# Hybrid decoder layer: the first expert choice made for one head, eight candidates ahead, and the causal mask of the first two token tiles added by VectorE

## The reference, cut to what matters

```python
h = rms_norm(x, norm1_g); proj = h @ w_in
A = stick_breaking_attention(q, k, v)     # 8 heads x 64, strictly causal
B = gated_deltanet(...)                   # 4 heads x 128, chunked
x = x + concat(rms_norm(A), B) @ w_out
h = rms_norm(x, norm2_g)
# PEER: per token 8 heads, each picks 16 of 128*128 experts
s1, s2 = q1 @ keys1.T, q2 @ keys2.T       # 128 scores each
v1, i1 = top_k(s1, 16); v2, i2 = top_k(s2, 16)
score, pos = top_k(v1[:, None] + v2[None, :], 16)
expert = i1 * 128 + i2 (at pos); gate = softmax(score)
x = x + sum over 8*16 experts of gate * gelu(h . u[expert]) * v[expert]
```

## Time and profile before

| | us |
|---|---|
| median of 3 runs | 1650.77 (1649.88 to 1652.06) |
| profiled execution, own time | 1653.62 |
| its span, first to last instruction | 1651.7 |
| PE busy | 1357.4 (82%) |
| DVE busy | 1057.7 (64%) |
| POOL busy | 776.3 (47%) |
| ACT busy | 349.9 (21%) |
| gathers: 115776 packets, 536.92 MB | 80.6% of 16 DMA engines' span |

### The profile page before, as it was taken

How to read it: one execution, slowest core, us unless ns; L and a number is a source line. 1 busy time by engine, 2 the same in 40 slices (tenths; PEclk the granted TensorE clock), 3 DMA queues, 4 the chain that set the end, 5 groups by cost and what they waited for, 6 DMA issues and landing times.

```text
span 1651.7 us, 15972 instructions
## 1 busy us (share of the span) xinstructions
PE 1357.4 (82%) x5078; PEld 675.1 (41%) x5078; DVE 1057.7 (64%) x2839; ACT 349.9 (21%) x786; POOL 776.3 (47%) x848
## 2 busy tenths in 40 slices
PE   8999989888789887977859976677877787778877
PEld 7866574433346555643213320122333333333333
DVE  4625249957777889976555766444565666666646
ACT  2321432302242322011002120021122222222221
POOL 3000015766676657765557677445433333333331
PEclk8999999999999898987879898799989999998899
DMA  4223817999999999999999999999999999999995
GB/s 155 77 102 115 303 41 273 389 410 412 409 409 409 411 410 409 409 409 412 399 413 409 378 410 411 418 418 416 421 422 421 422 421 422 421 422 421 422 422 241
DMA packets 130211, 599.35 MB, mean 363 GB/s; under 512 B 15824, under 2 KB 15824, under 8 KB 97360
## 3 DMA queue, kind: packets, MB, share of 16 engines
q0 software_dynamic: 115776, 536.92, 80.6%
q1 hardware_dynamic: 14208, 61.15, 9.7%
q10 hardware_dynamic: 144, 0.26, 0.0%
HBM read 596.18 MB, written 2.10 MB: 362 GB/s over the span
## 4 chain that ended last, share of the span: by engine, by line
DMA 45%; PE 28%; DVE 10%; POOL 8%; issue 5%; ACT 3%; DVEq 1%; ACTq 0%; SPq 0%; POOLq 0%
DMA arena<-in_peer_uv,arena 19%; DMA arena<-in_peer_v,arena 16%; DMA arena<-in_peer_u,arena 10%; PE psum L1153 7%; DVE arena L1954 4%; POOL arena L741 4%; POOL arena L753 4%; PE psum L1131 4%; PE psum L1084 3%; PE psum L817 3%; PE psum L828 3%; PE psum L1065 1%; DVE arena L1554 1%; ACT arena L1444 1%; PE psum L932 1%
## 5 line engine op out<-in xcount | busy, mean ns | idle before, releaser
L1954 DVE CUSTOM_DVE_ANT_0 arena<-arena,psum 128x1024 f32<-128x1024 f32 x512 | 623.3, 1218 | 418.6 <-DMA arena<-in_peer_uv,arena 247.0
L1153 PE MATMUL psum<-arena 128*128 128x512 f32 x880 | 427.3, 644 | 95.2 <-ACT arena L1444 95.2
L741 POOL DMA_INDIRECT arena<-in_peer_u,arena x288 | 273.7, 950 | 360.2 <-PE psum L894 223.0
L1131 PE MATMUL psum<-arena 128*32 128x512 f32 x1152 | 278.3, 719 | 134.7 <-DMA arena<-in_peer_v,arena 134.5
L773 POOL DMA_INDIRECT arena<-in_peer_uv,arena x220 | 206.3, 938 | 333.5 <-PE psum L1153 294.7
L753 POOL DMA_INDIRECT arena<-in_peer_v,arena x288 | 271.8, 944 | 143.3 <-issue 76.6
L1153 PEld LDWEIGHTS psum<-arena 128*128 128x128 f32 x880 | 176.3, 205 | 350.6 <-issue 219.2
L1131 PEld LDWEIGHTS psum<-arena 128*32 128x32 f32 x1152 | 48.0, 119 | 317.0 <-DMA arena<-in_peer_v,arena 230.2
L817 PE MATMUL psum<-arena 128*128 128x512 f32 x256 | 117.1, 604 | 1.3 <-DVE st L1596 1.2
L828 PE MATMUL psum<-arena 128*128 128x256 f32 x384 | 97.0, 414 | 5.7 <-ACT arena L1212 4.2
L1084 PE MATMUL psum<-arena 128*128 128x512 f32 x224 | 100.5, 602 | 1.3 <-ACT arena L1371 1.3
(11 more groups left out here) (283 smaller groups left out, 1392.1 us busy)
## 6 DMA issues: line engine op xcount, KB each, us to landing
arena<-in_w_in SPq DMA_DIRECT2D x28, 1024.0 KB, 7.8
arena<-in_w_out SPq DMA_DIRECT2D x16, 512.0 KB, 7.9
arena<-in_peer_w_q SPq DMA_DIRECT2D x16, 512.0 KB, 14.1
arena<-in_peer_w_q SPq DMA_DIRECT2D x8, 1024.0 KB, 13.3
arena<-in_peer_u,arena POOLq DMA_INDIRECT x292, 15.2
arena<-in_peer_v,arena POOLq DMA_INDIRECT x292, 15.9
arena<-in_peer_uv,arena POOLq DMA_INDIRECT x220, 27.1
arena<-in_x SPq DMA_DIRECT2D x4, 512.0 KB, 5.0
```

The lines of the kernel that those rows point to most:

```text
L741: pool.indirect_dma_start(row, None, u_d, bass.IndirectOffsetOnAxis(ap=eid[i % 2][:, c:c + 1], axis=0)).then_inc(landed, 16)
L1131: mm = pe.matmul(bank[6 + half][group * UK:(group + 1) * UK], zrows[k % 2][:, z0:z0 + ZW], row[:, half * 512:(half + 1) * 512], start=Fals ...
L1153: mm = pe.matmul(bank[y_bank[i][half]], diag_w[q % 2][:, j], row[:, D + half * 512:D + (half + 1) * 512], start=False, stop=c == SEL - 1 o ...
L1954: dve.tensor_tensor_reduce(row, row, h2p[i], 1.0, 0.0, ALU.mult, ALU.add, dots[:, c:c + 1]).then_inc(s["u_free"], 1)
```

## The change

- `z` for tiles 0 and 1: the product with the identity goes; the first product of the bank starts it, and DVE adds the mask to the diagonal block in PSUM (`mask`); ACT waits for that instead of for PE. Tiles 2 and 3 stay.
- The list of steps is rearranged: the masks stand where `z` stands in DVE's order; `st(0,0)` comes after `z(1,1)`, `r(1,0)` after `wo(0)`, `h2T` before `os(1,0)`. The first quarter of the query product and its scores are split by head: `q1`, `s1` (i = 0 for head 0, i = 1 for head 1), with head 1's half after `r(1,2)`.
- The choice of head 0 is split: `choose_first(0)` finds the best eight pairs from the eight best of either side and gives out eight expert ids (semaphore `eight`); `choose_first(1)`, later, finds the rest.
- `FIRST` is 10 with two more buffers (8 and 12 KB, where x tiles 2 and 3 lie), and the waits in `gather_u` are set anew; x tiles 2 and 3 are loaded after dot 1 instead of after the weight blocks. `on(1,0)` moves into the loop after dot 2, `add` and `n2` of tile 1 from row 8 to row 9.
- In the inverse's level 0, the products with the identity (L934, L951) become transposes.

```diff
-            ("o", 0, 0), ("os", 0, 0), ("o", 0, 1), ("osn", 0, 0), ("on", 0, 0), ("nw", 1, 0), ("st", 0, 0),
-            ("z", 1, 0), ("z", 1, 1), ("sp", 1, 0), ("sp", 1, 1), ("mix", 0, 0), ("mix", 0, 1), ("r", 1, 0),
-            ("wo", 0, 0), ("add", 0, 0), ("wo", 0, 1), ("add", 0, 1), ("n2", 0, 0), ("vn", 1, 0), ("z", 1, 2),
-            ("os", 1, 0), ("st", 1, 0), ("h2T", 0, 0), ("h2T", 0, 1), ("r", 1, 1), ("sp", 1, 2), ("z", 1, 3), ("q", 0, 0),
-            ("sp", 1, 3), ("s", 0, 0), ("choose", 0, 0), ("o", 1, 0), ("o", 1, 1), ("r", 1, 2), ("o", 1, 2),
-            ("r", 1, 3), ("o", 1, 3), ("osn", 1, 0), ("on", 1, 0)]
+            ("o", 0, 0), ("os", 0, 0), ("o", 0, 1), ("osn", 0, 0), ("on", 0, 0), ("nw", 1, 0),
+            ("z", 1, 0), ("z", 1, 1), ("st", 0, 0), ("mix", 0, 0), ("mix", 0, 1), ("sp", 1, 0), ("sp", 1, 1),
+            ("wo", 0, 0), ("add", 0, 0), ("wo", 0, 1), ("add", 0, 1), ("n2", 0, 0), ("vn", 1, 0), ("r", 1, 0), ("z", 1, 2),
+            ("h2T", 0, 0), ("h2T", 0, 1), ("os", 1, 0), ("sp", 1, 2), ("q1", 0, 0), ("st", 1, 0), ("s1", 0, 0), ("choose", 0, 0),
+            ("r", 1, 1), ("z", 1, 3), ("sp", 1, 3), ("choose", 0, 1), ("o", 1, 0), ("o", 1, 1), ("r", 1, 2), ("q1", 0, 1),
+            ("o", 1, 2), ("r", 1, 3), ("s1", 0, 1), ("o", 1, 3), ("osn", 1, 0), ("on", 1, 0)]
...
-HELD = {("st", 1, 0): 1, ("add", 1, 0): 8, ("add", 1, 1): 8, ("n2", 1, 0): 8}
+ON_AT = 2
+HELD = {("st", 1, 0): 0, ("on", 1, 0): ON_AT, ("add", 1, 0): 9, ("add", 1, 1): 9, ("n2", 1, 0): 9}
...
+    if kind in ("q1", "s1"):
+        return [0] if i else [(a, b)["qs".index(kind[0])]]
...
-        FIRST = 8
-        first_row = [at(k, D) for k in (122, 126, 174, 80, 84, 170, 178, 182)]
+        FIRST = 10
+        first_row = [at(k, D) for k in (8, 12, 80, 84, 174, 122, 126, 170, 178, 182)]
...
+            sp.wait_ge(s["u_free"], 2)
+            for t in range(GT, NT):
+                sp.dma_start(xs[:, t], x_d[:, t]).then_inc(x_in[t], 16)
...
-                if c % TOPK == 0:
+                if n == 8:
+                    pool.wait_ge(*linked(0, 0, 11))
+                elif n and c % TOPK == 0:
                     pool.wait_ge(*linked(i, c // TOPK, 11))
 
                 if n == 0:
+                    pool.wait_ge(s["eight"], 1)
+                elif n == 2:
+                    pool.wait_ge(*filled("st", 1))
+                elif n == 4:
+                    pool.wait_ge(*filled("z", 1, SBH // AT_ONCE[1] - 1))
+                elif n == 5:
                     pool.wait_ge(*filled("o", 1, SBH // AT_ONCE[1] - 1))
-                elif n == 3:
-                    pool.wait_ge(*filled("st", 1))
-                elif n == 5:
+                elif n == 7:
                     pool.wait_ge(s["on_rdy"], 2)
-                elif n == 6:
+                elif n == 8:
                     for half in range(2):
                         pool.wait_ge(*filled("mix", 1, half))
                 elif FIRST <= n < FIRST + UB - 1:

...
-                    pe.matmul(ps[:, t * w:width], ident[:], sb_mask.unsqueeze(1).to_broadcast([P, AT_ONCE[t], P]),
-                              start=True, stop=False, skip_group_check=True)
+                    if t >= GT:
+                        pe.matmul(ps[:, t * w:width], ident[:], sb_mask.unsqueeze(1).to_broadcast([P, AT_ONCE[t], P]),
+                                  start=True, stop=False, skip_group_check=True)
...
-                                           start=False, stop=False, skip_group_check=True)
+                                           start=t < GT and kb == 0 and hh == 0, stop=False, skip_group_check=True)
...
-                            mm = pe.matmul(a[:, cols[h]], AT_[t][:, h], ident[:], start=True, stop=True)
+                            mm = pe.transpose(a[:, cols[h]], AT_[t][:, h], ident[:])
...
+                elif kind == "q1":
+                    ps = claim("q1", 0, i)
+                    if i == 0:
+                        for a in range(2):
+                            pe.wait_ge(*read("h2T", 0, a))
+                        pe.wait_ge(s["wq_in"], 16 * DC)
+                    for j in range(2 * i, 2 * i + 2):
+                        for c in range(DC):
+                            mm = pe.matmul(ps[:, j * P:(j + 1) * P], w_q_h[0][c][:, j * HALF:(j + 1) * HALF], h2T[0][:, c],
+                                           start=c == 0, stop=c == DC - 1)
+                    mm.then_inc(filled("q1", 0, i)[0], 1)
+                elif kind == "s1":
+                    ps = claim("s1", 0, i)
+                    pe.wait_ge(*read("q1", 0, i))
+                    pe.wait_ge(s["keys_in"], 16)
+                    for j in range(2 * i, 2 * i + 2):
+                        mm = pe.matmul(ps[:, j * NKEYS:(j + 1) * NKEYS], qs[0][:, j], keysT[:, j], start=True, stop=True)
+                    mm.then_inc(filled("s1", 0, i)[0], 1)
...
+                    if g == 0:
+                        act.wait_ge(s["masked"], n + 1)
...
+                elif kind in ("q1", "s1"):
+                    act.wait_ge(*filled(kind, 0, i))
+                    two = slice(2 * i, 2 * i + 2)
+                    act.copy(qs[0][:, two], heads(bank_for(kind, 0, i))[:, two]).then_inc(read(kind, 0, i)[0], 1)
+                    if kind == "s1" and i == 0:
+                        load_h2(0)
...
+            def mask(t, i):
+
+                w = AT_ONCE[t] * P
+                diagonal = bank_for("z", t, i)[:, t * w:(t + 1) * w].rearrange("p (h q) -> p h q", q=P)
+                dve.wait_ge(*filled("z", t, i))
+                dve.tensor_tensor(diagonal, diagonal, sb_mask.unsqueeze(1).to_broadcast([P, AT_ONCE[t], P]), ALU.add
+                                  ).then_inc(s["masked"], 1)
...
+                elif kind == "z" and t < GT:
+                    mask(t, i)
...
-                    for link in range(LINKS):
-                        choose(0, 0, link)
+                    choose_first(i)
...
+            def choose_first(second):
+
+                scores = [qs[0][:, a] for a in range(2)]
+                pair_, pair_rest = crest[:, 0:64], crest[:, 64:128]
+                first = slice(0, 8)
+                if second:
+                    return choose_rest(scores, pair_, pair_rest, first)
+                dve.wait_ge(*read("s1", 0, 0))
+                for a in range(2):
+                    dve.max(top[:, a, first], scores[a])
+                dve.drain()
+                for a in range(2):
...
+                few = differ.rearrange("p a m n -> p (a m n)")[:, 0:128].rearrange("p (a m n) -> p a m n", a=2, m=8)
+                for a in range(2):
+                    dve.tensor_tensor(few[:, a], posk[:, a, first].unsqueeze(2).to_broadcast([P, 8, 8]),
+                                      code[:, a, first].unsqueeze(1).to_broadcast([P, 8, 8]), ALU.bitwise_xor)
...
+                dve.scalar_tensor_tensor(eid[0][:, first], ids[:, 0:8], float(NKEYS), ids[:, 8:16], ALU.mult, ALU.add
+                                         ).then_inc(s["eight"], 1)
+
+            def choose_rest(scores, pair_, pair_rest, first):
+
+                last = slice(8, 16)
...
+                dve.scalar_tensor_tensor(eid[0][:, last], ids[:, 0:8], float(NKEYS), ids[:, 8:16], ALU.mult, ALU.add
+                                         ).then_inc(s["linked"], LINKS)
```

72 lines of the change are left out of this document (58 added, 14 removed).

## The result

The changed kernel is slower: 1657.41 us (median of 14 runs, 1655.54 to 1662.94) against 1651.24 us for the kernel before beside it (14 runs, 1649.82 to 1655.34). The ratio is 1.0038, with a 95% interval of 1.0029 to 1.0047. The forecast was 1653.1, 2.3 us more than before, with "no difference" as the likeliest case. The time lies inside the range by 0.1 us, and the direction of the sum was right, but the interval leaves out "no difference", and the loss is 6.2 us where 2.3 was forecast. The profiled execution of the changed kernel has 1662.27 us of its own (span 1660.5), 8.65 more than the profiled one of before (span 1651.7).

A forecast was written before the change was run, and what follows sets the result against it. Full DMA queues bound the kernel from row 29 on, which hangs on wo(1) and DVE's dots. wo(1) +3.7, less 0.2 and 1.2, gave +2.3: median 1650.8 to 1653.1 us, range 1647.3 to 1657.5.

The forecast's parts named there:

- Rival (a): PE's holes before mix(0,1) and o(1,1): half clock costs 0.7 on wo(0) and 1.7 more, median 1655.5; chance 0.23.
- Part 1: Masks of tiles 0 and 1 on DVE: ACT starts z(1,0) 2.7 us later behind tile 0's norm, wo(0) starts 2.0 later.
- Tile 0's masks come out even: Tile 0's score steps: PE and DVE masks, both twice as wide, swap on the same path at no net cost.
- wo(0)'s duration: Tile 0's output product on PE: kept at today's 15.16 us, a stretch at half clock included.
- Part 2: End of wo(0) to first gather: 17.3 us, choice of eight 3.3 us; first gather at 230.2, 10 us earlier.
- Part 3: End of wo(0) to wo(1): 42.3 us with queue waits and the moved query half; wo(1) at 255.2, 3.7 later.
- Part 4: Gather rows after wo(1): early gathers give back one dot (1.2 us) and 0.2 of DVE lag; row 29 is 2.3 later.
- Rival (b): Gather rows: the head start pulls row 29 along, end up to 10 us earlier, 1641; chance whole or in part 0.12.
- the first gather is not on it: Chain to the end: it runs from wo(1) through DVE's block and dots 9 to 21 to row 29, without the first gather.
- Sum: Whole kernel: row 29 and the end 2.3 us later, profiled run 1655.9, median 1653.1.
- Edits at nothing: Later x loads, level 0 transposes and changed slot waits: no effect, bounds -0.5 to +0.5 us together.
- little more: Projection behind the level 0 transposes: a possible small loss from half clock, given no size.

The follow-up runs named there:

- e4: Changed kernel, masks still on DVE, with products of no use filling PE's holes before mix(0,1) and o(1,1); ratio to before 1.0019, stage 121.6 us.
- h2: Same kernel as e4, run again for its time; ratio to before 0.9943, stage 121.7 us.
- e3: Changed kernel with the first gather held until o(1,3) is done; ratio to before 1.0124, stage 138.2 us.
- g3: Changed kernel, on(1,0) done before dot 0, first gather held until ACT has copied q(0,1); 1668.58 us, stage 137.2 us.
- g0: Kernel before, unchanged, profiled once more; 1654.6 us, stage 118.6 us.
- e1: Changed kernel with the level 0 transposes made again by products with the identity; ratio to before 1.0052, stage 128.2 us.
- g1: Kernel before with only the four level 0 products with the identity turned into transposes; 1648.77 us, beside one run of before of 1650.48.
- f2: Changed kernel with masks on PE, level 0 by products, and products of no use before mix(0,1) and o(1,1); ratio to before 0.9982, stage 116.0 us.
- h3: Same kernel as f2, run again for its time; ratio to before 0.9998, stage 116.0 us.
- k1: Same kernel as f2, run a third time; ratio to before 1.0049, stage 115.9 us.
- f4: Kernel before with two products of no use in PE's 2.24 us hole before mix(0,1); ratio to before 1.0026, stage 122.6 us.

## Why the prediction was wrong, point by point

**The step that failed** is one term of the sum: the half clock behind the two holes of PE. The forecast saw both holes, kept wo(0) at 15.16 "which contains a stretch at half clock", and put nothing for it anywhere else. Measured against the forecast it was 0.5 us in mix(0,1), 1.7 in wo(0) and 3.3 behind o(1,1), 5.5 in all; the runs with the holes filled (e4, h2) take it back, together with the 1.2 us of half clock that wo(0) has in the kernel before too. Rival (a) named this mechanism, with a chance of 0.23, and sized it at 2.4.

**Part 1, masks.** The mechanism was right: ACT waits 2.66 us for a mask behind the norm, where 2.7 was forecast. "Tile 0's masks come out even" held, though not for the reason given. r(0,0) waits 1.90 for DVE and then runs at half clock (2.04 for 1.02), so that the norm of tile 0 ends 19.3 us after the first score product instead of 18.0; but the mask product ahead of it, 1.0, is gone, and from the first instruction of z(0,0) it is 19.3 against 19.0. wo(0) came 2.7 us later, counted so, not 2.0: 0.3 from tile 0, and 0.5 from mix(0,1), which ran at half clock (1.12 for 0.66).

**wo(0)'s duration** was kept at 15.16. It was 16.86, and 13.97 with the hole filled. "Which contains a stretch at half clock" was true, but with the hole grown from 2.24 to 5.40 wo(0) began at 0.50 and took more of the low stretch. Rival (a) had this mechanism, with 0.7 for it; it was 1.7.

**Part 2.** Right to 0.3 us: the first gather came 17.6 after wo(0)'s end (forecast 17.3), and the choice took 3.4 us from MAX8 to the eighth index, 230.97 to 234.38 (forecast 3.3).

**Part 3.** The sum from wo(0)'s end to wo(1), 42.3, is met to the tenth wherever PE stays at full clock (e4, h2), with the masks' hole before o(1,1) included (3.0, forecast 3.4). In the changed kernel 3.3 more came from half clock behind that hole: 0.87 in o(1,1), 0.94 and 0.47 in r(1,2), 1.07 in the second q1. Rival (a) said 1.7. Its argument against itself, that a wait of 1.25 us was followed by none, did not bear on a hole of 3 us.

**Part 4.** wo(1) to row 29 took 39.7, not 40.5. Early rows gave back 2.2 us instead of 1.4. Row 18, the first that needs the slot of a finished dot, waits 3.90 us for DVE, as row 17 waited 3.28 in the earlier trace rows. And DVE's block now waits for PE, as forecast (its timeline, 275 to 283, answers the earlier trace rows):

```profile
275.86 0.69 DVE L1859 TENSOR_TENSOR arena<-arena,psum 128x512 f32<-128x512 f32 x1 [4.99 <-PE psum L1059]
...
282.43 1.20 DVE L2068 CUSTOM_DVE_ANT_0 arena<-arena,psum 128x1024 f32<-128x1024 f32 x1
```

So slots and DVE, not choices, set the pace. Rival (b) is excluded: against wo(1), the head start moved row 29 by these 2.2 us and no more. But "the first gather is not on it" (on the chain to the end) holds in one direction only. Held back by 16.6 us against the end of wo(0) it delays wo(1) by 8.6, through dot 2 and on(1,0) (e3); with that norm out of the way and held back by 24.9, by 4.7, through dot 0 and st(1,0) (g3).

**Sum.** Forecast +2.3 for row 29. Measured +9.0, in two parts. The stage, from the first instruction of z(0,0), grew by 2.7 + 1.7 + 4.9 - 2.2 = 7.1 (8.6 against g0). From the forecast that is 2.3 + 5.5 of half clock + 0.3 of tile 0 - 0.8 from Part 4, 7.1 but for rounding. And z(0,0) began 1.9 later (174.14 for 172.25), of which 1.2 stood already at the start of level 0 of the inverse (67.11 for 65.94), before which none of the edits acts. Filling the holes takes back 6.6 of the 7.1; putting the masks on PE takes back 6.8 or 8.2, since it closes most of the holes too; both together 11.3. The rest of the change, freed of both, is 2.6 to 4.2 us shorter than before in the stage.

**Edits at nothing.** At full clock transposes cost and brought nothing (e1, g1); PE waits for DVE behind them as before (its timeline at 81, which answers the earlier trace rows):

```profile
81.38 1.16 PE L930 MATMUL psum<-arena 128*128 128x128 f32 x8 [1.48 <-DVE arena L1736]
```

The projection behind them did run at half clock in the profile after (5.98 us for 3.62), and of the 1.9 us some 0.65 arose here (14.27 us for 13.62 from the first step of level 0 to this wait). The rule of the Trainium skill (TensorE: Matmul & The Clock Gate, Part 4: PE-mode transpose) is that transposes don't count as activity for the clock as matmuls do. The traces agree where the clock fell: 6.8 us at half clock in four profiles with transposes, 3.4 in three with products. g1 had no fall and is no test of it. So the "little more" for which the prediction put nothing was 0.65 us in this profile. The loads of x were no cost that a row shows.

**What stays open.** The stage grew by 7.1 us, the medians lie 6.2 apart (interval 4.8 to 7.8). That fits, but against the other execution of before the stage grew by 8.6, and the projections before the stage scatter by several us between executions of either kernel, so it is not shown that the stage is the whole of the loss. The loss and its cure were measured in the stage alone; no whole time resolves them. Why ACT's copy of q(0,1) is late on one chip when gathers start beside it is open, too.

## What to carry to other kernels

Moving 0.6 us from one engine to another is priced by the queue it joins, not by its duration: look at what stands ahead of it there, and who waits. When such a wait opens a hole on PE, add what half clock costs behind it, against full clock 3.3 us here behind each of the holes of 5.4 and 3.0 us, before weighing a gain of the same size. And before calling a transfer off the path, ask which steps stand behind its consumer in the consumer's own order.

## What was not expected of the hardware

- Half clock depends on more than the length of a hole. With 2.24 us before mix(0,1), wo(0) took 15.0 us in one execution of the kernel before and 13.7 in another; with 1.90 us before r(0,0), half clock followed in all eleven executions with masks on DVE; with 1.20 us before o(1,1), one execution of the kernel with masks on PE ran from 227 to 234 at 0.76 and the other at 1.00 (42.3 and 40.7 us to wo(1)). The Trainium skill (TensorE: Matmul & The Clock Gate, HAM oscillation) tells of falls behind longer gaps; holes this short being followed by one is what these traces add.
- The stage repeats to 0.1 us, but its start does not: the first score product came between 168.2 and 175.1 us. In ten of the twelve executions that came to it between 168.2 and 170.2, the clock was 1.00 from 12 to 50 us (in g1 it was 0.62 over 12 to 16, in h2 0.67 over 20 to 24); in all eight that came to it at 173.2 or later it had been lower, in the profile of before (173.25) 0.50 to 0.82 over 12 to 28 us, in g0 (175.1) 0.50 to 0.85 over 20 to 32. The latest start did not have the longest low stretch, so that the clock is the cause is not shown. This scatter alone is larger than the effect of the change.
- Products of no use kept the clock up behind the wait that they filled: with PE busy through it, the clock stayed at 1.00 through wo(0) in each of the six profiles that had them (e4, h2, f2, h3, k1, f4). Behind waits left unfilled it still fell (r(0,0) in e4 and h2, o(1,1) in f4).
